# The norms between the phases in two halves of tokens, and GpSimd's share in them

## The reference, cut to what matters

```
for l in range(2):                                   # first block
    h = layer_norm(ALPHA*h + 0.5*swiglu(h, w_up, w_down), g, b)      # norm n = 3l
    h = layer_norm(ALPHA*h + hybrid_mixer(h, w_in, ...), g, b)       # norm n = 3l+1
    h = layer_norm(ALPHA*h + 0.5*swiglu(h, w_up, w_down), g, b)      # norm n = 3l+2
for l in range(2):                                   # second block, 256 tokens
    x = x + token_mixing(x, norm_g, w_in, ...)       # begins with rmsnorm(x, norm_g), ends with @ w_out
    h = rmsnorm(x, ffn_norm_g)
    x = x + (swiglu_2(h, ...) if l == 0 else moe_swiglu(h, w_router, ...))
return rmsnorm(x, final_norm_g)

layer_norm: (x - mean(x)) * rsqrt(var(x) + 1e-5) * g + b        # over the 1024 of a token
rmsnorm:    x * rsqrt(mean(x*x) + 1e-6) * g
swiglu:     (silu(x @ w_gate) * (x @ w_up)) @ w_down            # inner width 2816
```

## Time and profile before

| | us |
|---|---|
| median of 3 timed runs | 2655.45 (2654.16 to 2657.14) |
| profiled execution, span | 2653.2 |
| PE busy in the span | 2561.1 (97%) |
| DVE / ACT / POOL busy | 1943.4 / 1614.8 / 377.1 |
| last matmul before a norm to first of the next phase, 8 norms | 65.03 |

### The profile page before, as it was taken

The page is one execution under the profiler, slowest core; times in us unless marked ns, Lnnn a source line. Parts: engine busy times, 40 slices in busy tenths (PEclk is TensorE's granted clock), DMA queues, the critical chain, the costliest instruction groups (busy, mean ns, idle before and its releaser), DMA issues.

```text
span 2653.2 us, 65470 instructions
## 1 busy us (share of the span) xinstructions
PE 2561.1 (97%) x27736; PEld 2159.7 (81%) x27736; DVE 1943.4 (73%) x1886; ACT 1614.8 (61%) x1690; POOL 377.1 (14%) x440
## 2 busy tenths in 40 slices
PE   9999999999999999999999999999999999999998
PEld 8887788888887888897888888799778687787775
DVE  5467675564567765666765466689999999999997
ACT  4346653354357654455654446657888888887876
POOL 3211322121105221103021103031000000000000
PEclk9999999999999999999999999999999999999999
DMA  8574355555555655554455655378999999999996
GB/s 268 172 210 141 108 195 197 169 190 188 157 161 152 199 182 181 177 192 132 148 197 192 190 190 163 118 273 340 412 419 422 419 413 422 413 418 418 413 421 273
DMA packets 345255, 666.16 MB, mean 251 GB/s; under 512 B 20448, under 2 KB 273536, under 8 KB 306096
## 3 DMA queue, kind: packets, MB, share of 16 engines
q1 hardware_dynamic: 344192, 661.39, 69.0%
q0 software_dynamic: 528, 0.63, 0.3%
q10 hardware_dynamic: 288, 0.59, 0.1%
HBM read 661.49 MB, written 1.05 MB: 250 GB/s over the span
## 4 chain that ended last, share of the span: by engine, by line
PE 62%; DVE 19%; DMA 7%; ACT 6%; issue 4%; DVEq 2%; POOLq 0%; ACTq 0%; POOL 0%; SPq 0%
PE ps L2336 17%; PE ps L2338 17%; PE ps L2337 17%; DVE w_lo L1621 7%; DMA w<-in_moe_units 3%; DVE work L1621 2%; DMA mix<-in_moe_units 2%; DVE ff L1621 2%; DVE w_lo L1461 2%; ACT w_hi L958 2%; ACT w_hi L849 2%; DMA squares_and_low<-in_moe_units 1%; PE ps L2379 1%; PE ps L2385 1%; PE ps L2380 1%
## 5 line engine op out<-in xcount | busy, mean ns | idle before, releaser
L2336 PE MATMUL ps<-x_hi,w_hi 128*128 128x96 f16 (+2 forms) x5024 | 1076.1, 246 | 19.1 <-DVE w_lo L1621 5.8
L2338 PE MATMUL ps<-x_hi,w_lo 128*128 128x96 f16 (+2 forms) x5024 | 1075.4, 246 | 7.3 <-issue 7.3
L2337 PE MATMUL ps<-squares_and_low,w_hi 128*128 128x96 f16 (+2 forms) x5024 | 1075.5, 246 | 4.3 <-issue 4.3
L1461 DVE SCALAR_TENSOR_TENSOR w_lo<-w,w_hi 128x2048 f16<-128x2048 f32 (+4 forms) x335 | 680.8, 2043 | 295.0 <-ACT w_hi L849 293.2
L849 ACT ACTIVATE w_hi<-w 128x2048 f16<-128x2048 f32 (+4 forms) x335 | 556.8, 1671 | 85.7 <-PE ps L2338 74.8
L2336 PEld LDWEIGHTS ps<-x_hi,w_hi 128*128 128x128 f16 x5024 | 492.6, 98 | 76.0 <-issue 15.9
L2337 PEld LDWEIGHTS ps<-squares_and_low,w_hi 128*128 128x128 f16 x5024 | 492.6, 98 | 50.0 <-issue 5.3
L2338 PEld LDWEIGHTS ps<-x_hi,w_lo 128*128 128x128 f16 x5024 | 492.4, 98 | 49.1 <-issue 7.4
L2338 PE MATMUL ps<-ff,w_lo 128*128 128x272 f16 (+1 forms) x880 | 243.3, 276 | 0.0
L2337 PE MATMUL ps<-ff,w_hi 128*128 128x272 f16 (+1 forms) x880 | 243.3, 276 | 0.0
L2336 PE MATMUL ps<-ff,w_hi 128*128 128x272 f16 (+1 forms) x880 | 243.3, 276 | 0.0
(11 more groups left out here) (408 smaller groups left out, 4770.9 us busy)
## 6 DMA issues: line engine op xcount, KB each, us to landing
w<-in_ffn_w_up_units SPq DMA_DIRECT2D x176, 512.0 KB, 4.6
w<-in_moe_units SPq DMA_DIRECT2D x75, 1024.0 KB, 11.9
w<-in_moe_units SPq DMA_DIRECT2D x56, 1280.0 KB, 15.3
mix<-in_moe_units SPq DMA_DIRECT2D x50, 1024.0 KB, 12.0
w<-in_w_in SPq DMA_DIRECT2D x96, 512.0 KB, 4.8
mix<-in_moe_units SPq DMA_DIRECT2D x36, 1280.0 KB, 15.6
w<-in_mix_w_in SPq DMA_DIRECT2D x60, 512.0 KB, 5.0
squares_and_low<-in_moe_units SPq DMA_DIRECT2D x26, 1024.0 KB, 12.0
```

The source lines that it names most:

```text
L1461: vec.scalar_tensor_tensor(k.w_lo[:, s, 0:size], k.w32[:, s, 0:size], WS, k.w_hi[:, s, 0:size], ALU.mult, ALU.subtract).then_inc(k.parts_r ...
L2336: pe.matmul(acc, w_hi, x_hi, start=first, stop=False)
L2337: pe.matmul(acc, w_hi, x_lo, start=False, stop=False)
L2338: return pe.matmul(acc, w_lo, x_hi, start=False, stop=last)
```

## The change: what it does

All norms but the router's are cut at half of the tokens (136 or 128 columns; `part_of`).

- PE: the last two units of a down phase, and the last unit of wo and of wout of layer 0, are computed first for half 0 and then for half 1, into banks 6 and 7. The sums of half 0 stand 9 matmuls into half 1; the sums of half 1 stand inside the opening of the next phase, behind chunk 3. The opening (`opening_by_parts`) does all 8 chunks of half 0, then half 1, its low parts two chunks behind the high ones. `keep_warm` is gone.
- DVE: last chunk added, variance, reciprocal per half; chunks centred and multiplied by the reciprocal in pairs (two chunks of half the tokens in one instruction); the normed state is written to k.h at once, by one instruction a chunk and half. In rms norms the scaling stays chunk by chunk, in halves.
- ACT: its high part takes gain and bias in one; the later write to k.h is gone. The third unit's high part is split between the root of half 1 and the high parts of half 1.
- DVE splits the third unit behind the whole norm (in down phases it was before the last chunk); in wo and wout it splits the second unit directly behind chunks 4 and 5, before chunk 6 is out.
- POOL makes all low parts of the norms, in pairs (`low_parts`, `rms_low_parts`).

```diff
 # DVE, layer_norm (add_end, spread, centered, inverse act on half p)
+        def normed(p, pair):
+            th, c = part_of(t, p), slice(2 * pair, 2 * pair + 2)
+            vec.tensor_tensor(k.sq[:, c, th], k.h[:, c, th], over_pair(k.rstd[:, 0, th]), ALU.mult).then_inc(k.ln_scaled, 1)
+            if pair + 1 < PAIRS:
+                centered(p, pair + 1)
+            vec.drain()
+            for c in (2 * pair, 2 * pair + 1):
+                a = vec.tensor_scalar(k.h[:, c, th], k.sq[:, c, th], column(k, g0 + c), column(k, b0 + c), ALU.mult, ALU.add)
+            a.then_inc(k.h_normed, 1)
+        add_end(0)
+        vec.drain()
+        spread(0)
+        centered(0, 0)
+        inverse(0)
+        normed(0, 0)
+        normed(0, 1)
+        add_end(1)
+        normed(0, 2)
+        spread(1)
+        normed(0, 3)
+        centered(1, 0)
+        inverse(1)
+        for pair in range(PAIRS):
+            normed(1, pair)
+        if following is not None:
+            split(following + 2, q, UNIT)
 # DVE, wo_norm
         add_pair(2, False)
-        vec.wait_ge(k.wo_half, n // 3 + 1)
-        vec.tensor_tensor(k.h[:, 6, t], k.h[:, 6, t], k.ps[:, 0, t], ALU.add).then_inc(k.wo_half_out, 1)
         split(g + 5, q, UNIT)
 # DVE, rms_norm
+        add_end(0)
+        inverse(0)
+        normed(0, 0, 4)
+        add_end(1)
+        normed(0, 4, KC)
+        inverse(1)
+        normed(1, 0, KC)
+        if following is not None:
+            split(following + 2, 0, UNIT)
 # ACT, layer_norm (high: two activations of one chunk and half, Identity with scale and bias)
+        squares_of_end(0)
+        rest_square(0)
+        root(0)
+        high(0, 0)
+        high(0, 1)
+        squares_of_end(1)
+        high(0, 2)
+        rest_square(1)
+        high(0, 3)
+        root(1)
         if following is not None:
             split(following + 2, q, UNIT)
+        for pair in range(PAIRS):
+            high(1, pair)
 # POOL
+    def low_parts(n):
+        for p in range(2):
+            th = part_of(kept(n), p)
+            for pair in range(PAIRS):
+                c = slice(2 * pair, 2 * pair + 2)
+                pool.wait_ge(k.x_hi_ready, high_before(n, False) + KC * p + 2 * pair + 2)
+                pool.wait_ge(k.h_normed, 2 * PAIRS * n + PAIRS * p + pair + 1)
+                pool.tensor_tensor(k.x_lo[:, c, th], k.h[:, c, th], k.x_hi[:, c, th], ALU.subtract).then_inc(k.x_ready, 1)
 # PE, opening_by_parts (OPEN_TOGETHER 5, LAG 2, SUMS_AT 3)
+        for p in range(2):
+            for kc in range(OPEN_TOGETHER if p else KC):
+                high(p, kc, range(2))
+                if kc >= LAG:
+                    low(p, kc - LAG, range(2))
+                if (p, kc) == (0, SUMS_AT) and second_sums is not None:
+                    second_sums()
+            if p == 0:
+                for kc in range(KC - LAG, KC):
+                    low(p, kc, range(2))
+        for j in range(2):
+            for kc in range(OPEN_TOGETHER, KC):
+                high(1, kc, [j])
+            for kc in range(OPEN_TOGETHER - LAG, KC):
+                a = low(1, kc, [j])
+            a.then_inc(k.unit_done, 1)
```

More of the change, by code:

```diff
@@ L336, in over_units_early @@
     u0 = phase.units - AHEAD - 1
-    for u in range(phase.units):
+    for u in range(phase.units - 1):
         for n in (u + AHEAD,) if u < u0 else (u + AHEAD, u + AHEAD + 1) if u == u0 else (u + AHEAD + 1,):
@@ L962, in wout_squares @@
         root_ready()
-        for c in range(KC):
+        for c in range(KC if l == DEPTH - 1 else 6):
             if l == DEPTH - 1 and c == 0:
@@ L1345, in act_program @@
         if l == 0:
-            rms_norm(2 * l + 1, s["up"])
+            rms_norm(2 * l + 1, 6, s["wout"].base + 2 + 4, s["up"].first)
             up(s["up"], 0, 0, s["up"].gates, ALL2)
@@ L1496, in down, with last_unit_used @@
         over_units_early(phase, q, split, take)
+    def last_unit_used(phase, q):
+        vec.wait_ge(k.unit_done, q * SLOTS + (phase.first + phase.units + SLOTS))
     def add_first(m, t):
@@ L2358, in all_out, with opening @@
         pe.wait_ge(k.act_evac, act)
-    def opening(phase, q, evac, evac0, x_hi, x_lo, t, chunk, n_step, kc_step, late=False, both=TOGETHER, first_banks=(0, 2)):
+    def opening(phase, q, evac, evac0, x_hi, x_lo, t, chunk, n_step, kc_step, banks=(0, 2)):
         weights(phase.first, q)
-        if not late:
-            weights(phase.first + 1, q)
-        banks, free = first_banks, 1 if late else 2
-        pe.wait_ge(evac, evac0 + (phase.base + free))
+        pe.wait_ge(evac, evac0 + (phase.base + 1))
         def tile(j, n, kc):
@@ L2573, in rms_norm @@
-    def rms_norm(n, summed):
-        pe.wait_ge(k.squares_summed, 3 * DEPTH + n)
-        rms_sum(k.prod[:, 0, 0:T2], first=True)
-        for c in range(summed, KC):
-            pe.wait_ge(k.rms_squared, n * KC + c + 1)
-            a = rms_sum(k.sq[:, c, 0:T2], last=c == KC - 1)
-        a.then_inc(k.rms_mean, 1)
-        keep_warm()
+        opening(phase, q, k.vec_evac, vec0, k.x_hi, k.x_lo, t, chunk, P, 256, (2, 0))
+        g = phase.first + 2
+        weights(g, q)
+        pe.wait_ge(k.vec_evac, vec0 + 2 + (phase.base + 1))
@@ L2583, in turn_rows @@
+        for half in range(2):
+            a = chain(k.ps[:, 2 + half, t], g % SLOTS, [(kc * 256 + half * P, P, kc) for kc in range(KC)], k.x_hi[:, :, t], k.x_lo[:, :, t])
+            if half == 0:
+                shift(n)
+        a.then_inc(k.unit_done, 1)
+        last_unit_by_parts(phase, q, k.x_hi, k.x_lo, t, lambda: end_sums(n, 0, 6, None))
     def turn_rows(first, last):
@@ L2605, in wout_norm @@
     def wout_norm(n, l, phase, x_hi, x_lo, chunk):
-        opening(phase, 0, k.vec_evac, 0, x_hi, x_lo, ALL2, chunk, P, 256, True)
-        for u in (2, 3):
+        opening(phase, 0, k.vec_evac, 0, x_hi, x_lo, ALL2, chunk, P, 256)
+        for u in (2, 3) if l == DEPTH - 1 else (2,):
             g = phase.first + u
```

547 lines of the change are left out of this document (308 added, 239 removed).

## The result

The changed kernel takes 2669.67 us (median of 4 runs, 2665.56 to 2673.32) against 2655.52 for the kernel before; the ratio is 1.0055, 95% interval 1.0043 to 1.0068. Forecast were 2667 and slower. A second measurement, beside two experiments, gave 2667.74 and 1.0047 (1.0033 to 1.0061). Its profiled execution has a span of 2667.6 us, 14.4 above; the medians lie 14.15 apart.

The account below looks back on a forecast made before the run. PE, busy 97%, bounds the kernel; 2.1 + 2.6 + 1.95 + 2.1 + 2.6 + 1.0 - 0.6 + 0.1 = +11.85 us over eight norms make the span 2665.05, the median 2667 (8 in 10: 2643 to 2678).

Parts of the forecast that it names:

- The wait for half 0's sum: Norm 0: PE, in order, waits 1.44 us for ACT's square of half 0, 9 matmuls into half 1.
- t = 22.29: Norm 0: end of POOL's last low part, in us since PE had issued half of the last output.
- POOL's price per pair: Pairs of chunks in the norms: POOL's low parts add 0.24 us to DVE (bounds 0 and 0.56), giving 1.51.
- my 1.27: DVE's us per pair without POOL's price: product 0.35, centring 0.35, drain 0.17, two writes to k.h 0.20 each.
- The exclusion: Norms: DVE and POOL shut each other out while DVE has two SBUF operands or a fast float32 scaling.
- rival 4: Without fillers the clock falls to 1.2 GHz behind a stall of each norm: 13 us on top, 2680; chance 0.1.
- the eight stretches: One per norm, from half of the last output issued to the next opening's end; no change expected outside them.
- Rival 1: Ends of norms: POOL's last low part gets in before DVE's split; +4.7 us in all, 2660; chance 0.12.
- Rival 2: Pairs and the split behind them: no exclusion worth the name, low parts at 0.7; -8.0 us, 2647; chance 0.22.
- Rival 3: All norms: the halves hide the chain altogether, PE's work alone is left; -34 us, 2621; chance 0.06.
- +2.6 each: Norms 1 and 4 (wo): POOL's sum of chunks 4 and 5 waits for DVE's split; bounds -0.5 and +4.
- rms 1, +1.0: Norm behind wout: the split lies on POOL's squares, holding POOL to 3.1; 19.97 us for 19.00.

Follow-up runs that it names:

- experiment 5: Changed kernel with all low parts on DVE (first kernel): 1.0038; second kernel, also with the second unit's split behind half 0's last chunk: 0.9994.
- experiment 1: Changed kernel, but DVE's split of the third unit waits for POOL's last low part in all seven norms with low parts: 1.0013, 2658.87 us.
- experiment 3: Changed kernel with the second unit's split behind half 0's last chunk and the third unit's behind POOL's last low part: 0.9973, 2647.76 us.
- experiments 3, 4 and 8: 4: experiment 3's kernel, but DVE makes the last low part: 0.9957. 8: that plus 4 fillers between the opening's halves at layer norms: 0.9956.
- experiment 2: Changed kernel, but DVE splits the second unit behind half 0's last chunk instead of ahead of it, in all norms: 1.0013, 2659.24 us.

## Why the prediction was right, and where it was not

**The direction and the size**: +14.15 us measured, +11.85 forecast. The links named are there, but the number owes something to luck, to two errors that offset each other: the chain costs less than forecast, and the clock, which the forecast left out, makes up for it. By one of its own signs the forecast was wrong: the phases between the norms were to change by no more than 2 us and changed by 2.45, at a clock under 1.00 in two of them.

**PE's stalls.** The wait for half 0's sum was put at 1.44 and is 1.24; in half 0 of the opening 0.88 was forecast and some 0.3 came; between and in the pairs of half 1 2.02 were forecast, 0.98 + 0.33 + 0.39 = 1.70 came; for the last low part 2.57 forecast, 2.13 found. The forecast low part ended at t = 22.29, the measured at 21.46, and the opening at 23.07 and not 23.98.

**The step that was mis-sized** is POOL's price per pair: "Per pair I add 0.24 to DVE", giving 1.51. A pair takes 1.39 with POOL and without it (experiment 5), so the addition was 0.00. The 0.12 over my 1.27 are the two writes to k.h, 0.52 in the rows there and not 0.40; centring and drain take 0.51, as forecast (0.52). The addition came from the 494 ns of the earlier trace rows read as what each instruction pays beside POOL. It is a mean of eight unlike ones (shortest, median, longest, in ns):

```profile
L1625 DVE TENSOR_SCALAR ff<-h,col x8: 341/354/1032, 1771.0 to 1782.6; 128x256 f32<-128x256 f32 x8
```

Six of them take 0.34 to 0.36 us, four of these while POOL is at work, and two take 0.82 and 1.03: a mean over a group hid that most paid nothing. Of the 0.83 us by which the last low part came early, 0.54 are the four pairs of half 1. The low parts of ordinary pairs take 0.70 to 0.97 us. The exclusion decides only where DVE holds long, in the 2.3 us splits. Without the clock, by the stretches of the kernel with fillers in the stalls, the eight norms changed by +1.2, +2.75, +1.05, +1.2, +2.9, -0.2, -0.2 and -1.45, in the order of the earlier trace rows with the unshown one fourth: +7.2 against the +11.85 of the sum. Right in order and all but two in sign.

**The clock** was rival 4, at a chance of 0.1 and 13 us on top. It is there, at some 7 us. I gave its mechanism too little weight, and said that no row showed what follows without fillers. One did, outside the eight stretches: the token mixing of the second layer, with its 0.50 behind a stall with no filler, shown above. The stretches told the rest: a gap of 6.66 us held 3 us of fillers, and taking them out left stalls of 2 us and more uncovered. The 1.5 to 4 us a norm of the rival stood on no row; where the clock fell the two profiles show 1.0 to 2.0 us lost at a place. It falls by chance, too: of the two profiles of the changed kernel one has it at norm 2, the other at norms 1, 3, 4 and rms 2, both at rms 1.
The Trainium skill, "TensorE: Matmul & The Clock Gate", section "Part 1: The HAM clock gate", has an idle TensorE put back to 1.2 GHz; the traces agree (0.53 behind 2.4 us, 0.52 behind 4.28) and add that behind stalls of 2 us it happens in some executions and not in others.

**Rival 1** (POOL gets in ahead of the split) is refuted by the 2.61 us of the last low part, at 207.45 behind a split begun at 207.23. **Rival 2** (no exclusion) holds for the pairs and fails at the splits. With the last split alone out of the way the kernel stays at 1.0013 (experiment 1), far from the rival's 2647; that time is reached only with the other split moved as well (experiment 3, 2647.76). **Rival 3** is far off.

**wo and wout.** +2.6 each was forecast for the stretches of norms 1 and 4, and +2.75 and +2.84 came, in a profile with no fall of the clock there; rms 1, +1.0, came out at -0.2 without the clock and +0.8 with it. At norm 2 the changed kernel lost 4.5 us in its first profile. The split ahead of it waited 2.2 us for its DMA, which it did not in the second profile nor in that of the kernel with fillers in the stalls (in experiment 1's it did, 2.0 us, and the clock fell there too); this made the stall 1.4 us longer, and the longer stall was followed by a low clock.

## What to carry to other kernels

When work is cut finer to shorten a chain, look at what stands ahead of its first link and behind its last on the same in-order engine: here two long splits, each moved by one place, turned 1.0055 into 0.9973, and 0.9957 with DVE making the last low part. Give GpSimd work only where DVE's neighbouring instructions are short, and never have it owe a result while DVE begins a long one with two SBUF operands. Before fillers are taken out, count how long the matmul engine will then stand still. Before a mean over a group is read as a price, look at its shortest, median and longest.

## What the runs showed of the hardware that was not expected

- The exclusion between DVE and POOL is not felt in a mixed stream: pairs of DVE took 1.39 us with or without POOL, and POOL 0.76 us in it, but 2.61 and 2.59 beside one 2.3 us split. The one place where DVE paid regularly was the last pair of half 1, with two scalings and no centring between: 0.81 us instead of 0.61, the latter with no POOL beside it (experiment 5, first kernel).
The Trainium skill, "SBUF — State Buffer", section "SBUF: two separate sides", speaks of a lock held for a whole instruction; the runs agree, and show that its price is about what is left of the other's instruction: the last low part, begun with 2.06 us of the split to go, took 1.91 longer.
- In the changed kernel and its variants the clock fell to 1.2 GHz behind stalls of 2.1 to 2.7 us in some executions and not in others, and at none of norms 0 to 4 where their stalls were 1.3 us at most (experiments 3, 4 and 8). The kernel before shows that this is no safe bound: its fall at 1680 us stands behind an idle time of 1.71.
- Falls between 1200 and 1280 us, in the token mixing, stand in eight of the thirteen profiles (also in the fastest kernel's), with an idle time of 1.71 us ahead of one of them that the kernel before has too, without a fall. They are not in the profiles of before, of both kernels with fillers at the norms' stalls, of the one without the old fillers, nor of experiment 2. In the second layer's mixing the same idle time is followed by a fall in the kernel before. No experiment was made on them, and what decides is open.
